# The first four modulations of a two-part network, shared between TensorE and VectorE, with the norm behind them modulated in two parts

## The reference, cut to what matters

```python
c_act = jax.nn.silu(c)                                   # 1 x 1024
sh1, sc1, g1, sh2, sc2, g2 = split(c_act @ w_mod[0] + b_mod[0], 6)   # w_mod[0]: 1024 x 6144
h = modulate(rmsnorm(x, a_norm_g[0]), sh1, sc1)          # rmsnorm(x) * g * (1 + sc1) + sh1
proj = h @ w_in                                          # 1024 x (3 * 1024 + 16): q, k, v, forget logits
```

## Time and profile before

| | us |
|---|---|
| median of 3 runs | 2782.95 (2777.13 to 2792.56) |
| the profiled execution, its own time | 2783.22 |
| its span | 2781.4 |
| PE busy | 2528.6 (91%) |
| DVE busy | 1684.2 (61%) |
| ACT busy | 1312.1 (47%) |
| DMA, mean over the span | 194 GB/s |

### The profile page before, as it was taken

The page is one execution under the profiler, slowest core; times in us unless marked ns, Lnnn a source line. Parts: engine busy times, 40 slices in busy tenths (PEclk is TensorE's granted clock), DMA queues, the critical chain, the costliest instruction groups (busy, mean ns, idle before and its releaser), DMA issues.

```text
span 2781.4 us, 33080 instructions
## 1 busy us (share of the span) xinstructions
PE 2528.6 (91%) x13554; PEld 2166.7 (78%) x13554; DVE 1684.2 (61%) x1485; ACT 1312.1 (47%) x1758; POOL 93.9 (3%) x119
## 2 busy tenths in 40 slices
PE   4988999998778999998999999889998799999999
PEld 4867777787667777777977997679976699887898
DVE  6757887884556877774644555645556555644554
ACT  3545776433342756643343444444445344444443
POOL 1000000000000000000000000100000000000000
PEclk9998999998898999998999999989998999999999
DMA  8614999983522879873554594325543255563553
GB/s 284 229 61 151 342 345 341 320 279 99 182 72 75 303 267 328 285 289 117 186 166 136 185 259 165 121 78 197 191 140 121 86 196 193 165 199 123 167 188 130
DMA packets 231302, 539.90 MB, mean 194 GB/s; under 512 B 21072, under 2 KB 29808, under 8 KB 231152
## 3 DMA queue, kind: packets, MB, share of 16 engines
q1 hardware_dynamic: 208992, 471.82, 49.6%
q0 software_dynamic: 15520, 59.77, 6.1%
q10 hardware_dynamic: 6640, 6.20, 1.2%
HBM read 533.54 MB, written 4.19 MB: 193 GB/s over the span
## 4 chain that ended last, share of the span: by engine, by line
PE 66%; DVE 15%; DMA 8%; ACT 6%; issue 3%; POOL 1%; SPq 1%; ACTq 0%; DVEq 0%; POOLq 0%
DVE w_low L1945 6%; PE pair L930 6%; PE pair L932 6%; PE pair L938 6%; PE Y L1041 5%; PE Y L1043 5%; PE Y L1051 5%; PE pair L960 4%; PE pair L961 4%; PE pair L966 4%; DMA raw<-in_exp_w_down 3%; ACT w_high L1551 3%; DMA raw<-in_exp_w_gate 3%; PE pair L1243 2%; PE pair L1244 2%
## 5 line engine op out<-in xcount | busy, mean ns | idle before, releaser
L1945 DVE TENSOR_TENSOR w_low<-raw,w_high 128x2048 fp32r<-128x2048 f32 (+3 forms) x456 | 1022.2, 2247 | 686.6 <-ACT w_high L1551 681.9
L1551 ACT ACTIVATE w_high<-raw 128x1024 fp32r<-128x1024 f32 (+3 forms) x912 | 912.0, 1038 | 832.1 <-PE Y L1051 229.1
L930 PE MATMUL pair<-hT_high,w_high 128*128 128x256 f32 x1280 | 314.8, 286 | 14.3 <-DVE hT_low L2001 14.3
L932 PE MATMUL pair<-hT_low,w_high 128*128 128x256 f32 x1280 | 314.0, 285 | 0.0
L960 PE MATMUL pair<-w_high,hT_high 128*128 128x512 f32 (+2 forms) x644 | 253.9, 396 | 18.0 <-DVE hT_low L2001 10.2
L930 PEld LDWEIGHTS pair<-hT_high,w_high 128*128 128x128 f32 x1280 | 248.4, 194 | 17.1 <-DVE hT_low L2001 15.7
L961 PE MATMUL pair<-w_high,hT_low 128*128 128x512 f32 (+2 forms) x644 | 252.4, 393 | 0.0
L932 PEld LDWEIGHTS pair<-hT_low,w_high 128*128 128x128 f32 x1280 | 248.5, 194 | 0.9
L1043 PE MATMUL Y<-w_high,gated_low 128*128 128x512 f32 x528 | 205.8, 390 | 0.0
L1041 PE MATMUL Y<-w_high,gated_high 128*128 128x512 f32 x528 | 205.8, 390 | 0.0
L1287 PE MATMUL Y<-w_high,gated_high 128*128 128x512 f32 x320 | 133.9, 419 | 38.2 <-DVE gated_low L2251 33.1
(11 more groups left out here) (353 smaller groups left out, 3711.5 us busy)
## 6 DMA issues: line engine op xcount, KB each, us to landing
raw<-in_exp_w_gate SPq DMA_DIRECT2D x128, 512.0 KB, 4.6
raw<-in_exp_w_up SPq DMA_DIRECT2D x128, 512.0 KB, 4.9
raw<-in_exp_w_down SPq DMA_DIRECT2D x128, 512.0 KB, 4.7
raw<-in_w_up SPq DMA_DIRECT2D x128, 512.0 KB, 4.6
raw<-in_w_down SPq DMA_DIRECT2D x128, 512.0 KB, 4.4
work<-in_w_mod POOLq DMA_DIRECT2D x48, 1024.0 KB, 7.8
raw<-in_ret_w_in SPq DMA_DIRECT2D x96, 512.0 KB, 4.7
raw<-in_ret_w_out SPq DMA_DIRECT2D x32, 512.0 KB, 4.4
```

What stands on the lines that cost most here:

```text
L930: nc.tensor.matmul(ps[:, f, :], high[:, k, f * P:(f + 1) * P], hT_high[:, kk, :], start=(kk == 0 and f % 2 == 0), stop=False)
L932: nc.tensor.matmul(ps[:, f, :], high[:, k, f * P:(f + 1) * P], hT_low[:, kk, :], start=False, stop=False)
L1551: nc.scalar.activation(w_high[:, s % HIGH, part], raw[:, s % RAW, part], ACT.Copy).then_inc(high_ready, 1)
L1945: V.tensor_tensor(w_low[:, s % HIGH, 0:n], part, w_high[:, s % HIGH, 0:n].bitcast(F32), ALU.subtract).then_inc(low_ready, 1)
```

## The change

1. PE takes half the depth of the four first modulations straight from the weights: for weight blocks k = 0 to 3 of each (and 6 and 7 of modulation 3) it makes four products with the 128 x 128 weight as the stationary operand and `c_act[:, k]` as the moving one, into the same 4 columns of PSUM. DVE makes the running sum of blocks 4 to 7 only (4 and 5 for modulation 3), and PE adds it as before by products with ones.
2. The order is 0, 2, 1, 3 for the loads, for PE and for DVE.
3. The gain is made in two parts. After modulations 0 and 2 the first four feature blocks can be modulated by ACT and split by DVE, while 1 and 3 are still being made; the last four follow.
4. SP waits for `first_loaded[7]` instead of `[5]`; its wait for step 4 of modulation 0 is gone. POOL waits until PE has finished all four products, instead of for DVE's steps of modulation 1, before it loads modulations 4 to 7.
5. ACT feeds piece 0 before it copies the thin sums.

```diff
+FIRST_ORDER = (0, 2, 1, 3)
+FIRST_STEPS = (4, 4, 4, 2)
...
         def wait_mod(eng, m, steps):
-            eng.wait_ge(mod_step, 8 * m + steps)
+            if m < FIRST_MODS:
+                eng.wait_ge(mod_step, sum(FIRST_STEPS[:FIRST_ORDER.index(m)]) + steps)
+            else:
+                eng.wait_ge(mod_step, sum(FIRST_STEPS) + 8 * (m - FIRST_MODS) + steps)
...
-            sp.wait_ge(first_loaded[5], 16)
+            sp.wait_ge(first_loaded[2 * FIRST_MODS - 1], 16)
             load_range(0, 1)
             load(1, source(plan.streamed[1]), (0,))
-            wait_mod(sp, 0, 4)
             for dst, src in needed_later:
...
             for i in range(2 * FIRST_MODS):
-                pool.dma_start(first_raw[:, i], layer_mod(i // 2)[:, 4 * (i % 2):4 * (i % 2) + 4]).then_inc(first_loaded[i], 16)
+                src = layer_mod(FIRST_ORDER[i // 2])
+                pool.dma_start(first_raw[:, i], src[:, 4 * (i % 2):4 * (i % 2) + 4]).then_inc(first_loaded[i], 16)
             pool.wait_ge(half_ready, 1)
             inverse_rms(plan.a_norm.stat)
-            wait_mod(pool, 1, 8)
+            pool.wait_ge(modulated, FIRST_MODS)
             load_mods(STAGES["a"])
...
             def first_modulation(m):
-                mod_product(m, first_mods[m]).then_inc(modulated, 1)
+                at = FIRST_ORDER.index(m)
+                late = 4 + FIRST_STEPS[at]
+                for k in (*range(4), *range(late, KD)):
+                    if k in (0, late):
+                        pe.wait_ge(first_loaded[2 * at + k // 4], 16)
+                    for f in range(4):
+                        nc.tensor.matmul(first_mods[m][:, f:f + 1], first_raw[:, 2 * at + k // 4, k % 4, f * P:(f + 1) * P],
+                                         c_act[:, k:k + 1], start=(k == 0 and f == 0), stop=False)
+                wait_mod(pe, m, FIRST_STEPS[at])
+                for f in range(4):
+                    last = nc.tensor.matmul(first_mods[m][:, f:f + 1], mod_total(m)[:, f * P:(f + 1) * P], ones_col,
+                                            start=False, stop=(f == 3))
+                last.then_inc(modulated, 1)
...
+            pe.wait_ge(c_ready, 1)
             first_modulation(0)
-            first_modulation(1)
-            def the_other_two():
-                first_modulation(2)
-                first_modulation(3)
-            other_half = norm(plan.a_norm, the_other_two)
+            def the_others():
+                for m in FIRST_ORDER[1:]:
+                    first_modulation(m)
+            other_half = norm(plan.a_norm, the_others)
...
-            def norm_high(n, g, shift=None, tmp=None):
+            def norm_high(n, g, shift=None, tmp=None, gains=None):
                 for j, use in enumerate(n.uses):
+                    if gains is not None:
+                        se.wait_ge(gains, j + 1)
                     wait_full(se, use)
...
-            se.wait_ge(first_gain, 1)
-            norm_high(plan.a_norm, gain, MOD[0] + SH1, v_area)
+            norm_high(plan.a_norm, gain, MOD[0] + SH1, v_area, first_gain)
+            feed(1)
             copy_thin(plan.f_logit, 0)
             feed(HIGH)
...
-            def norm(n, g, shift=None, tmp=None):
+            def norm(n, g, shift=None, tmp=None, between=None):
...
                 for j, use in enumerate(n.uses):
+                    if j and between is not None:
+                        between()
...
             def first_bias(m):
-                ve.wait_ge(modulated, m + 1)
+                ve.wait_ge(modulated, FIRST_ORDER.index(m) + 1)
                 link(add_bias(m, first_mods[m]))
+            def first_rows(m):
+                at = FIRST_ORDER.index(m)
+                ve.wait_ge(first_loaded[2 * at + 1], 16)
+                for i in range(FIRST_STEPS[at]):
+                    part, c_k = first_raw[:, 2 * at + 1, i], c_act[:, 4 + i:5 + i]
+                    if i == 0:
+                        V.tensor_scalar(mod_total(m), part, c_k, None, ALU.mult).then_inc(mod_step, 1)
+                    else:
+                        wait_mod(ve, m, i)
+                        V.scalar_tensor_tensor(mod_total(m), part, c_k, mod_total(m), ALU.mult, ALU.add).then_inc(mod_step, 1)
+            def gain_part(j):
+                ks = slice(4 * j, 4 * j + 4)
+                V.scalar_tensor_tensor(gain[:, ks], mod[:, SC1 + 4 * j:SC1 + 4 * j + 4], 1.0, cols[:, A_G + 4 * j:A_G + 4 * j + 4],
+                                       ALU.add, ALU.mult).then_inc(first_gain, 1)
             ve.wait_ge(c_ready, 1)
-            mod_rows(0)
+            first_rows(0)
             wait_full(ve, plan.columns)
             empties(plan.columns, V.tensor_copy(cols[:], pair(plan.columns)[:, 0:2 * P]))
             wait_emptied(ve, plan.columns)
-            mod_rows(1)
+            scale_rows(plan.a_norm)
+            first_rows(2)
             first_bias(0)
-            scale_rows(plan.a_norm)
-            mod_rows(2)
-            first_bias(1)
+            first_bias(2)
+            gain_part(0)
             ve.wait_ge(thin_high_made, 1)
             V.tensor_tensor(thin_low[:, 0], thin[:, 0], thin_high[:, 0].bitcast(F32), ALU.subtract).then_inc(thin_ready, 1)
-            mod_rows(3)
-            first_bias(2)
-            first_bias(3)
-            V.scalar_tensor_tensor(gain[:], mod[:, SC1:SC1 + KD], 1.0, cols[:, A_G:A_G + KD],
-                                   ALU.add, ALU.mult).then_inc(first_gain, 1)
-            norm(plan.a_norm, gain, SH1, v_area)
+            first_rows(1)
+            def second_gain():
+                first_rows(3)
+                first_bias(1)
+                first_bias(3)
+                gain_part(1)
+            norm(plan.a_norm, gain, SH1, v_area, second_gain)
```

More of the change, by code:

```diff
@@ L1956, in mod_half @@
                 for k in range(4 * h, 4 * h + 4):
[L1957 to L1964, removed]
+                    part = mod_raw(m, h)[:, k % 4]
+                    if k % 4 == 0:
+                        ve.wait_ge(mod_loaded[mod_slot(m, h)], 16 * mod_turn(m, h))
                     if k == 0:
```

## The result

The changed kernel takes 2800.05 us (median of 18 runs, 2782.52 to 2816.12), the kernel before 2783.26 us (18 runs, 2769.83 to 2793.44): ratio 1.0062, 95% interval 1.0042 to 1.0082, so 12 to 23 us slower. The forecast was 2801, slower.

What follows compares the result with a forecast made beforehand. DVE was taken to bound the first stage, with PE's half-clock price deciding: + 18.4 - 1.7 + 0.8 + 2.2 - 1.6 = +18.1 us on 2783.22, forecast 2801. The case's own range was 2794 to 2809; 2783 to 2809 covered about 8 in 10.

Steps and rivals of the forecast that it cites:

- The price: PE's new one-column products: 0.43 us each at half clock, from the nearest rows; the other end 0.225.
- the granted clock's first full stretch only around 70: Sign in the changed profile: PE's granted clock is first at full for a stretch only around 70 us.
- rival C: PE's clock rises midway, for example at 29.7 behind the transposes; 2783 to 2785, no change; chance 0.07.
- the term of +18.4: PE at the end of modulation 3: row ends at 58.9 instead of 40.5, 18.4 us later.
- near 39 and 59: Sign in the changed profile: ACT's first four L1586 operations near 39 us, the last four near 59.
- The split norm: Norm in two parts: first half hidden under PE's modulation 3, half the thin product saved; gives back 1.7 us.
- Behind the copy: Thin product and first projection on PE: small products 0.8 us more, clock's rise under the projection 2.2 us more.
- Slack: Before the second projection: ACT's copy follows PE at once, at 81.2, where PE had waited 1.73 us; -1.6 in the sum.
- The sum: Total up to the second projection: + 18.4 - 1.7 + 0.8 + 2.2 - 1.6 = +18.1 us, carried to the end.
- SP and POOL: Later waits of SP's transfers and POOL's loads cost nothing; the thirteen issued by 53.4; without cover, one load of 2.7 us.
- rival B: PE's clock rises under the long row of new products; -3 us, 2780, not slower; chance 0.12.

Runs made afterwards that it cites:

- e1: Changed kernel with DVE making all eight blocks of each first modulation again, 16 narrow products on PE; 2783.18 us, ratio 1.0006 to the kernel before.
- e2: Kernel before with PE's share alone (88 narrow products), old order, norm in one part; 2796.31 us, ratio 1.0058 to the kernel before.
- e4: Changed kernel with PE's share cut to blocks 0 and 1 of each modulation, 48 narrow products; 2781.55 us, ratio 1.0021 to the kernel before.
- e5: Changed kernel with PE making all eight blocks of each first modulation, 128 narrow products; 2814.57 us, ratio 1.0115 to the kernel before.
- e10: Changed kernel with 42 unused 128-column products on x ahead of the narrow row; 2793.18 us, ratio 1.0035 to the kernel before.
- e3: Changed kernel with each of the 88 products made with 128 equal moving columns instead of one; 2787.81 us, ratio 1.0030 to the kernel before.
- e7: Changed kernel with 18 unused 128-column products on x before the parameters arrive; 2793.98 us, ratio 1.0037 to the kernel before.
- e8: Changed kernel again, unaltered, with a second profile; 2800.67 us, ratio 1.0050 to the kernel before.
- e9: e6 with PE's blocks of modulation 0 made ahead of the small parameters' transposes; 2777.37 us, ratio 0.9975 to the kernel before.
- e6: Changed kernel with 64 wide products, three-block PE share, modulation 1 sums earlier, filler products on PE; 2784.01 us, ratio 0.9993 to the kernel before.

## Why the prediction was right

*The mechanism.* PE's share of narrow products, at half clock, makes the loss: without it the loss is gone (e1), alone it is there (e2), and it grows with the number of products (e4, e5).

*The price.* 0.43 us a product was the first choice, with 0.225 as the other end. Modulations 0, 1 and 3 paid it; the row of e5 and the windows of e10 confirm it. The rule of the Trainium skill's page "TensorE: Matmul & The Clock Gate" (Part 1: The HAM clock gate), that activity releases the throttle, agrees with e3, whose clock came up under the row, and not with the changed kernel: PE is busy for all 22.5 us from 32.3 to 54.8 at 0.50.

*What failed in the forecast's sum.* The step "the granted clock's first full stretch only around 70" was wrong. There was one at 28.9, behind the transposes, and the same in e2, e4, e5, e7, e8 and e10. It moves with the transposes: in e2 and e5, where they end at 38.0 and 34.7 and not at 29.0, it began at about 38.8 and 34.6. No run leaves them out, so what raised the clock stays open. The stretch took 3.4 us at double pace, so the row ended at 54.9, not 58.9, the start 0.5 us earlier included. This is a piece of rival C, whose rise came at the named place but did not last. So the term of +18.4 measured 14.3 (54.8 against 40.5). The stretch also put ACT's first four blocks at 34.95 and its last four at 55.43, not near 39 and 59.

*The split norm.* Half the thin product gave back 1.9 us, 1.7 as put: from the last product's slot to the copy are 61.35 - 54.79 = 6.56, against 8.41 before. DVE's first half, its steps and the scaling of the rows were indeed hidden; DVE waited 25.7 us.

*Behind the copy.* The small products at half clock cost 0.8, and the first projection took from 63.59 to 76.15, 12.6 instead of 11.2: +1.4, not +2.2. The clock came back sooner than I had assumed.

*Slack.* 1.6 us were to be regained before the second projection: ACT copied at 76.19 as soon as PE had ended, as forecast, with piece 3 ready at 73.5; 1.5 were regained.

*The sum* at the second projection was forecast at +18.1 and is 14.3 - 1.9 + 0.8 + 1.4 - 1.5 = +13.1 in the first profile; the second has +13.9. The medians say +16.8 and +17.0, with intervals of 12 to 23 and 6 to 22 us. So that the forecast's 2801 lies 1 us from the median is partly luck: the sum was 4 to 5 us too high at the place where it was made, and the medians stand 3 to 4 us above what the stage shows. Both intervals hold the stage's value; whether the rest is noise or a small cost behind the stage is open.

*SP and POOL* cost nothing here, as put: SP had issued the thirteen by 45.4 (53.4 had been put), and the 69.2 us from the second projection to the first attention are unchanged. e9 shows at what point SP's part would decide, which the prediction's working named only as a bound of rival B.

## What to carry to other kernels

Idle time on TensorE is no free resource for products with one moving column. Each is two records of the profile, each with a 128-column weight load of its own, and over rows of them without a gap the granted clock stood at 0.50, for 22.5 us in the changed kernel and 34.3 in e5. So price them at the half-clock step of the nearest such row, even where the row is long. With 128 equal columns a product cost no more at the same clock, and the clock then held at 1.00: the price was half. What a stage gains is read at the start of the first stage that is dense behind it, over several profiles; whether the kernel gains is for the medians alone to say. Here they confirmed the stage's loss, gave back 8.5 us of e3's 13.1, and did not show e6's 6.7 at all.

## What the hardware showed that I had not expected

- The windows of the kernel before give a granted clock of 1.00 for its first 49 us, but the durations in them are those of half clock: sixteen transposes took 3.65 us at 26.33, and 1.91 us in e3 at 24.57, behind wide products.
- A clock that was up fell at the end of a gap of 3.55 us (e3, at 46.2), and fell 2.2 us into a gapless row with one moving column (e10).
- The first attention's clock differs by chance: 0.72, 0.85 and 0.91 in three executions, 10 us between two of the same kernel. The part of the span behind the second projection went from 2701 to 2731 us over the profiles, and not in step with the number of narrow products.
- One small transfer of 128 partitions held SP for 3.29 us in one run of e6's kernel and 5.84 in another.
